# A decoder trunk layer: two products ahead of a norm's last sum, a query tile ahead of the sample's index stage, and values turned in two banks

## What is computed

```python
h = x + 0.5 * g1 * swiglu(modulate(x, g_ffn1, s1, sc1), w1_gate, w1_up, w1_down)
n = modulate(h, g_mix, s2, sc2)              # RMS norm, then shift and scale per sequence
z = n @ w_in                                 # conv GLU | q | k | v | indexer q, k, weights | gates
A = silu(layernorm(causal_conv31(glu(z)))) @ w_conv_out
I[t, s] = sum_h w[t, h] * relu(q_idx[t, h] . k_idx[s])       # keep the top 256 (sample: top 65) keys
B = softmax_attention(q, k[top], v[top]) @ w_attn_o          # sample: keys and values in cache pages
h = h + g2 * ((sigmoid(g_c) * A + sigmoid(g_a) * B) @ w_out)
h = h + 0.5 * g3 * swiglu(modulate(h, g_ffn2, s3, sc3), w2_gate, w2_up, w2_down)
y = rmsnorm(h, g_final)                      # also returned: rotated k, v, indexer k, conv state
```

## Time and profile before

| | |
|---|---|
| median of 3 runs | 2723.54 us (2717.31 to 2726.49) |
| the profiled execution: its time, its span | 2726.95 us, 2724.6 us |
| PE busy, DVE, POOL, ACT | 94%, 48%, 34%, 22% of the span |
| mean granted TensorE clock | 0.965 of full speed |
| chain that ended last | PE 72%, DVE 18%, issue 4%, ACT 3% |

### The profile page before, as it was taken

How to read it: one execution, slowest core, us unless ns; L and a number is a source line. 1 busy time by engine, 2 the same in 40 slices (tenths; PEclk the granted TensorE clock), 3 DMA queues, 4 the chain that set the end, 5 groups by cost and what they waited for, 6 DMA issues and landing times.

```text
span 2724.6 us, 41950 instructions
## 1 busy us (share of the span) xinstructions
PE 2552.8 (94%) x15990; PEld 2372.9 (87%) x15990; DVE 1302.6 (48%) x2420; ACT 598.7 (22%) x1079; POOL 918.6 (34%) x490
## 2 busy tenths in 40 slices
PE   5999999999999878899998769899899999999998
PEld 3899999999998846799997436889799999999997
DVE  4333333333334637799998345451533333333333
ACT  2310011101102323312334367310401111001103
POOL 1123323322233225546997010123133333333332
PEclk8999999999999979999999869999999999999999
DMA  8322222222220522221225500343011111111111
GB/s 278 109 78 77 70 77 77 69 69 77 77 77 21 149 76 72 77 97 48 87 94 169 180 1 1 95 136 100 16 47 47 44 44 44 45 46 46 46 54 64
DMA packets 208658, 209.93 MB, mean 77 GB/s; under 512 B 14143, under 2 KB 161715, under 8 KB 207657
## 3 DMA queue, kind: packets, MB, share of 16 engines
q1 hardware_dynamic: 198380, 181.70, 21.1%
q10 hardware_dynamic: 10181, 26.90, 3.1%
HBM read 173.03 MB, written 28.94 MB: 74 GB/s over the span
## 4 chain that ended last, share of the span: by engine, by line
PE 72%; DVE 18%; issue 4%; ACT 3%; SPq 2%; DMA 1%; POOL 1%; DVEq 0%; ACTq 0%; POOLq 0%
PE main L248 21%; PE main L249 21%; PE main L250 21%; DVE junk L1128 6%; DVE aux L1333 3%; DVE pick L1282 2%; PE main L1684 1%; PE main L1701 1%; PE aux L1712 1%; SPq L1467 1%; PE aux L983 1%; PE main L336 1%; PE aux L336 1%; ACT tmp L452 1%; PE aux L394 1%
## 5 line engine op out<-in xcount | busy, mean ns | idle before, releaser
L248 PE MATMUL main<-nhi,whi 128*128 128x352 f32 x3192 | 1042.5, 327 | 23.4 <-DVE nlo L464 20.0
L249 PE MATMUL main<-nlo,whi 128*128 128x352 f32 x3192 | 1029.2, 322 | 0.0
L250 PE MATMUL main<-nhi,wlo 128*128 128x352 f32 x3192 | 1028.2, 322 | 0.0
L235 POOL CAST whi<-raw 128x1024 fp32r<-128x1024 f32 x185 | 196.7, 1063 | 1586.7 <-PE main L250 1271.4
L248 PEld LDWEIGHTS main<-nhi,whi 128*128 128x128 f32 x3192 | 602.5, 189 | 56.6 <-issue 44.0
L249 PEld LDWEIGHTS main<-nlo,whi 128*128 128x128 f32 x3192 | 603.6, 189 | 0.6
L250 PEld LDWEIGHTS main<-nhi,wlo 128*128 128x128 f32 x3192 | 602.0, 189 | 0.6
L237 POOL TENSOR_TENSOR wlo<-raw,whi 128x1024 fp32r<-128x1024 f32 x185 | 461.7, 2496 | 14.8
L686 DVE TENSOR_TENSOR tmp<-main,tmp 128x352 f32<-128x352 f32 x132 | 69.3, 525 | 779.5 <-PE main L250 776.4
L705 DVE SCALAR_TENSOR_TENSOR h<-main,ada,h 128x352 f32<-128x352 f32 (+1 forms) x528 | 296.8, 569 | 114.7 <-PE main L250 114.7
L248 PE MATMUL main<-hid_hi,whi 128*128 128x352 f32 x1056 | 342.8, 325 | 0.0
(11 more groups left out here) (300 smaller groups left out, 2413.3 us busy)
## 6 DMA issues: line engine op xcount, KB each, us to landing
ada_raw<-in_w_ada SPq DMA_DIRECT2D x18, 2048.0 KB, 9.4
raw<-in_w_gate SPq DMA_DIRECT2D x44, 512.0 KB, 3.7
raw<-in_w_up SPq DMA_DIRECT2D x44, 512.0 KB, 3.8
raw<-in_w_down SPq DMA_DIRECT2D x44, 512.0 KB, 3.6
raw<-in_w_in SPq DMA_DIRECT2D x40, 512.0 KB, 3.6
gate_d<-zraw ACTq DMA_DIRECT2D x16, 528.0 KB, 2.7
gates<-gate_d SPq DMA_DIRECT2D x16, 528.0 KB, 4.6
zsw<-zraw ACTq DMA_DIRECT2D x42, 132.0 KB, 2.4
```

Source lines behind the costliest of these rows:

```text
L235: pool.tensor_copy(hi, raw[:, slot]).then_inc(hi_done, 1)
L248: pe.matmul(bank, w_hi[:, w], hi(c), start=(i == 0), stop=False)
L249: pe.matmul(bank, w_hi[:, w], lo(c), start=False, stop=False)
L250: last = pe.matmul(bank, w_lo[:, w], hi(c), start=False, stop=(i == n - 1))
```

## The change

Three places change; all three keep the work as it is and move it, or its buffers.

**The norm's end.** PE runs chunk 0 of tiles 0 and 1 before the last `gather` instead of behind it, with a wait for the FFN's last use of their banks, and `total` directly behind the `gather`. ACT does the last chunk's `root` before the second half of `affine` of chunk 1, and the conditioning's copy (`act_ada`) behind that half. DVE does the first half of the last chunk's `scale` ahead of the second half of chunk 1's `low`.

**Tile 5.** PE multiplies all three chunks of tile 5 before the sample's index stage, which then waits for tile 5's evacuation from PSUM too. ACT evacuates and swaps tile 5 (after DVE's rotation of tile 4) ahead of its work for the index stage. SP loads tile 5 ahead of the rotary tables. The index scores begin with tile 6.

**The turns.** The nine value tiles are turned in the two banks `main` 2 and 3 alternately instead of four; each turn from the third on waits for the copy two before it, and the wait for the whole convolution ahead of them is gone. The keys' turns use four banks again; the first that takes an `aux` bank (g = 10) waits for `CV_TOTAL - LEFT`.

```diff
         def mixer_pe_end(pe):
             norm_wait(pe, "m", "sd", 2)
             pe_ada(pe, ADA_LAST, 1, INIT_ADA // 8 + NPAIR, aux[:, 1])
+            norm_m["ready"](pe, 0)
+            for L in range(2):
+                ffn_wait(pe, "1", "down_free", 24 * NPAIR + 19 + 3 * L)
+                z_product(pe, L, T_Z + L, L % RING, None, L % 2, 72 if L == 0 else P, ts=(0,))
             norm_m["gather"](pe, 2)
+            norm_m["total"](pe, 2)
...
             m["affine"](act, 1, 0)
+            m["root"](act, 2)
+            m["affine"](act, 1, 1)
             act_ada(act, ADA_LAST, aux[:, 1], ada_rows[2])
-            m["affine"](act, 1, 1)
-            m["root"](act, 2)
...
             m["inverse"](dve, 2)
+            m["scale"](dve, 2, 0)
             m["low"](dve, 1, 1)
-            m["scale"](dve, 2, 0)
             m["scale"](dve, 2, 1)
...
-            n = 2 * (6 * (L - Z_Q) + 2 * t + half)
-            return range(n, n + 2) if L >= Z_Q and n < len(PIECES) else range(0)
+            n = 2 * (6 * (L - Z_Q - 1) + 2 * t + half)
+            return range(n, n + 2) if L > Z_Q and n < len(PIECES) else range(0)
...
-            for L in range(3, Z_Q):
-                load_tile(sp, T_Z + L, L % RING, cols(w_in, ZCOL[L]))
+            for L in range(3, Z_Q + 1):
+                load_tile(sp, T_Z + L, (T_Z + L) % RING, cols(w_in, ZCOL[L]))
             norm_wait(sp, "m", "lo", 6)
...
-            for L in range(Z_Q, NZ):
+            for L in range(Z_Q + 1, NZ):
                 load_tile(sp, T_Z + L, L % RING, cols(w_in, ZCOL[L]))
...
         def m1_pe(pe):
-            for t in range(NTC):
+            for t in range(1, NTC):
                 for L in range(2):
                     norm_m["ready"](pe, t)
                     z_product(pe, L, T_Z + L, L % RING, 3 * L, L % 2, 72 if L == 0 else P, ts=(t,))
-                    if (L, t) == (0, 0):
-                        norm_m["total"](pe, 2)
-                    if (L, t) == (1, 0):
+                    if (L, t) == (0, 1):
                         pe_ada_turn(pe, ADA_LAST, aux[:, 1], ada_rows[2])
             for L in range(2, Z_Q):
                 z_product(pe, L, T_Z + L, L % RING, 3 * L, L % 2)
 
-            pe.wait_ge(z_free, 6 + 3 * Z_Q)
+            z_product(pe, Z_Q, T_Z + Z_Q, (T_Z + Z_Q) % RING, 3 * Z_Q, Z_Q % 2)
+            pe.wait_ge(z_free, 6 + 3 * Z_Q + 3)
             pe.wait_ge(state_in, 32)
...
-            for L in range(Z_Q, Z_LOOP):
+            for L in range(Z_Q + 1, Z_LOOP):
...
+            act.wait_ge(rope_a, 3 * Z_Q)
+            evac(act, zrow(Z_Q), Z_Q, ACT.Copy, None)
+            act.wait_ge(z_free, 6 + 3 * Z_Q + 3)
+            swap(act, Z_Q, P)
             for g in range(2):
                 act.wait_ge(st_t, g + 1)
...
-            act.wait_ge(rope_a, 3 * Z_Q)
-            for L in range(Z_Q, Z_GLU):
+            for L in range(Z_Q + 1, Z_GLU):
...
         def turn_bank(g):
+            if g < 9:
+                return main[:, 2 + g % 2]
             return (main[:, 2], main[:, 3], aux[:, 0], aux[:, 1])[g % 4]
...
                 n = P if t < 8 else NSAMP
-                if g >= 4:
-                    pe.wait_ge(kv_e, g - 3)
+                if g >= 2:
+                    pe.wait_ge(kv_e, g - 1 if g < 10 else g - 3)
+                if g == 10:
+                    pe.wait_ge(cv, CV_TOTAL - LEFT)
...
             pe.wait_ge(v_in, 16)
-            pe.wait_ge(cv, CV_TOTAL)
             for t in range(9):
                 turn_tokens(t, vraw, t)
```

More of the change, by code:

```diff
@@ L918, in z_product @@
             for t in ts:
-                pe.wait_ge(z_free, V + t + 1)
+                if V is not None:
+                    pe.wait_ge(z_free, V + t + 1)
                 product(pe, main[0:m, 3 * parity + t, 0:TC], slot, range(KD),
```

## The result

The changed kernel takes 2702.75 us (median of six runs, 2697.85 to 2709.93), the kernel before beside it 2721.7 us (six runs). The ratio (of the means of these runs) is 0.9935, with a 95% interval of 0.992 to 0.9951: 17.7 us faster, 13.3 to 21.8 by the interval. The forecast of 13.6 us less lies at its lower edge. The two profiled executions, 2726.95 and 2709.43 us, differ by 17.5.

What follows compares the result with a forecast made beforehand. PE sets most of the span, DVE a stretch; SP's chain releases the prompt's attention. Tile 5 -11.45, index stage -0.95, SP's pause -1.2: together -13.6 us, predicted 2710 us, range 2702 to 2719.

Steps and rivals of the forecast that it cites:

- The norm's end: Last gather at full clock, last `low` near 909.4; PE gains 2.4 us, SP 6.2, its indexer pages ending near 949.3.
- Tile 5 and the index stage: Tile 5 fills the 13.88 us wait, 11.4 us off PE's path; first index matmul at 973.2, stage 0.95 us early.
- late rotation: Rival: tile 4's rotation ahead of the index stage as late as before, 6.6 us late at worst, 2717.5 us; chance 0.16.
- full clock: Rival: index stage runs at the full clock, its matmuls take half, some 7 us of 14.89 busy, 2703 us; chance 0.12.
- The products' end: Product tiles beside DVE's chain: they end 12.4 us earlier, 11.4 from tile 5 and 0.95 from the index stage.
- The turns: Values' turns end near 1501.6; value pages start near 1504.4, SP's pause 1.2 us less, PE's wait ends at 1548.7.
- DVE's end: End of DVE's index scores, threshold search and convolution: only 0.95 us earlier, at 1508.
- 18 us of cover: Layer norm, which still needs the convolution, comes near 1526, 18 us behind DVE's end, so DVE delays nothing there.

Runs made afterwards that it cites:

- index_pipelined: Changed kernel with the index stage's first two pages transposed first, each page one sequence ahead of its matmul, other transposes between, ACT's copies first; ratio to before 0.9885.
- norm_tile: Norm's edit and tile 5 on the kernel before; values' turns still in four banks behind the whole convolution; 2726.3 us.
- values_early: Changed kernel with SP's load of the values ahead of the key pages of sequences 4 and 5; ratio to the kernel before 0.9951.
- pages_ahead: Changed kernel with the sixteen page numbers read into registers during the last product tiles; ratio to the kernel before 0.9916.
- turns_alone: Kernel before with only the values' turns in two banks and without the convolution's wait; ratio to the kernel before 0.9991.

## Why the prediction was right, step by step

**The norm's end: right.** The gather took 1.39 us at the full clock behind 1.28 us of idle, the last `low` ended at 909.24 (forecast 909.4), PE idled 7.20 us and lost the clock (0.50 from 896.90 to 907.14), and SP's pages ended at 949.2 (949.3). What the prediction did not say is how little this is worth: without it the kernel is as fast, within what can be told.

**Tile 5 and the index stage: right.** The rotation began at 960.24 (961), with one instruction of 3.32 us beside POOL's subtract and the others 1.25: 5.8 us and not 3.8, which cost next to nothing, since tile 5's last product ended at 966.7 and its evacuation, which waits for both, at 967.24 (forecast 967.4). The first index matmul came at 973.06 (973.2), the stage took 19.69 us at the half clock as before, and ended 1.06 us early (0.95). The *late rotation* and the *full clock* did not come: behind 3.94 us of idle the stage ran at 0.50. That is also what the prediction had from a rule of the Trainium skill ("TensorE: Matmul & The Clock Gate", Part 1), and the trace agrees. index_pipelined shows that the full clock was to be had with the same work in a busier order.

**The products' end: 1 us more than forecast.** 13.4 us early (1475.44 to 1462.04, PE's first row behind the products) instead of 12.4: the granted clock in the stretch with the scores was 0.95 instead of 0.93. The prediction had no term for this; the seven traces of this order give 13 to 16 us.

**The turns: right.** 12.47 us of wait, ended by the values' transfer; value pages from 1503.05 (1504.4), 14.9 us early and so 1.5 more than the products (1.2); the second half of the sample's attention at 1546.89 (1548.7), 15.4 us early (13.6). The remaining 2 us of the 17.5 came in the prompt's attention and behind it, where no operation differs.

**The step that failed: DVE's end.** "DVE's chain ends only 0.95 us earlier, at 1508", with 18 us of cover: it ended at 1518.46, and the cover was 6.2 us at the layer norm and 2.3 at the first key turn. The prediction carried DVE's chain over as a block, moved by the index stage's shift. But tile 5 left the stretch with the scores and POOL's rotations did not move along with DVE: the flips came 2.3 us earlier and the rotation beside them 3.9, so that the first six met it. The Trainium skill ("SBUF — State Buffer", Who interferes with whom) says that a plain `tensor_scalar` can take the port pair that DVE shares with GpSimd, that its accumulating form does not, and that an instruction with two SBUF inputs waits for GpSimd's reads. The runs agree on all three: 12.68 us instead of 3.06 for six, 1.27 for 1024 columns beside POOL's rotation, and 12.67 and 16.81 for six with two inputs. The prediction used this rule for the rotation only. norm_tile shows what the third part of the change was worth because of it: the first two alone make the kernel slower. That the forecast held is luck in part: 6.2 us of cover were left where it counted 18, and 2.3 at the key turns. The length of the flips hangs on tenths of a us: POOL's rotation began 0.64 us behind the first flip here, 0.70 and 0.72 in values_early and pages_ahead, and there the same six flips took 10.5 us.

**The size.** Forecast 13.6, measured 17.7 (13.3 to 21.8). Of the 17.5 us between the two profiled executions, the products' end gave 1.0 more than forecast, the stretch up to the sample's second half 0.8 more, and 2.1 came behind it, where the forecast had nothing; their cause is open.

## What to carry to other kernels

A tile moved into a wait shifts two chains by different amounts, and whatever they share meets at a new time; go through the second chain's instructions by what the neighbour engine does beside them at the new time, and write elementwise steps there in the form that does not wait (its worth where DVE bounds was not run: in the changed kernel it was nothing that can be told). A wait of a few us ahead of a stage of short matmuls can cost more by the clock than by itself, so an order that keeps PE busy (the next page's transpose ahead of this page's matmul) may be worth more than the wait: 3.94 us of wait here, and 14.4 us gained at the stage's end. Where a queue reads a page number before each transfer, read the numbers ahead: 0.83 us a page instead of 2.6 here.

## What the runs showed of the hardware

*The clock in the first 60 us.* The profiled executions differ by some 8 us before the first changed instruction (start in the table: 872.6 to 874.2, or 881.1 to 883.3). The same 130 matmuls near the start, in the kernel before and in turns_alone (windows):

```profile
30.32:61.23 30.91, 25.09 (x130) 8.87 (x123) 13.73 (x10) 8.92 (x13) 7.04 (x5) 0.67 0.74 247
```

```profile
30.64:53.07 22.43, 16.58 (x130) 6.55 (x123) 13.64 (x10) 8.93 (x13) 2.51 (x2) 0.96 0.82 261
```

Nothing in the program differs there. The gap is nearly half of the whole spread of the kernel before (2712.6 to 2730.9 us over 29 runs), so a single execution's time tells nothing finer than that.

*Reading a page number.* On SP it takes some 1.8 us (2.6 for a page with it, 0.83 without), and behind a load of 2.1 MB the next page came 7.1 us after the load was issued (values_early), though SP had nothing else to wait for that the trace shows.
